# A two-layer hybrid backbone with a mixture of experts: the layout of the expert weight slots in SBUF

## The chip, the cores and the metric

The kernel runs on one core of a Trainium2 chip. The metric is the device time in microseconds of one execution, the median of three. Five engines work beside each other on the core, each with its own stream of instructions: TensorE (PE: matmuls and turnings, with PEld for its weight loads), VectorE (DVE), ScalarE (ACT), GpSimd (POOL) and SyncE (SP, which issues nearly all transfers). 16 DMA engines move the data. The engines wait for each other on semaphores.

## The reference

All data are fp32. There are 256 latent tokens and 256 context tokens of width 1024, and two layers. In each layer:

```
h  = modulate(rms_norm(x, g_mix), sh1, sc1)       # six modulation vectors = silu(c) @ w_ada + b_ada
z  = h @ w_in                                     # conv, two attentions, three gates
x += gt1 * (sum_i sigmoid(gate_i) * (o_i @ w_branch_i)) @ w_out
h2 = modulate(rms_norm(x, g_ffn), sh2, sc2)
aff = softmax(h2 @ w_router)                      # 16 experts; each picks its best 32 tokens of 256
xe = h2[idx]                                      # (expert, 32, 1024)
a, u = xe @ w_exp_gate[e], xe @ w_exp_up[e]       # 1024 x 1024 each, as is w_exp_down
ye = ((silu(a) * u) @ w_exp_down[e]) * gate       # added back to the tokens that were picked
x += gt2 * ye
```

The first layer does this for the latent and the context tokens, the second for the latent ones alone. The result is `rms_norm(x, g_final)` of the latent tokens.

## The kernel before

`make_plan` writes one list of steps for each layer, and every engine walks the same list and does its part of each step. Up to the experts a layer is dense work: `w_ada` and `w_in` blocks come through a ring in SBUF; each block is split into two fp32r parts (`WH`, `WL`, lines 1008 and 1183) and multiplied three times (lines 1535 to 1537).

The step `moe` is the expert stage. One expert has three matrices of 1024 x 1024, 4 MiB each. They are loaded as six slots of 2 MiB (`SLOT` is 4096 words on each of 128 partitions): slots 0 and 1 hold w_exp_gate, 2 and 3 w_exp_up, 4 and 5 w_exp_down. In a slot, partition p holds rows p, 128 + p, 256 + p and 384 + p of the 512 rows, 4 KiB each. SP loads the six slots of expert 0 while the dense work ends (line 874), then, in a loop over the experts 1 to 15, waits for `chunk_used[j]` and loads slot j again (line 878). All of these transfers lie in one queue, in that order.

TensorE (line 1641 on) takes the experts four at a time (`g`), with `eo` from 0 to 3 inside. `product` multiplies the gathered tokens (`XEB`, the stationary operand) with the rows of a slot, which stream past as the moving operand, and counts `chunk_used[j]` up at a slot's last matmul. G column groups of the array work at once, each on 1024 / G columns of the result: G is 2 in layer 0 (64 token slots, latent and context) and 4 in layer 1 (32 token slots). After gate and up, ScalarE and VectorE form silu(a) * u in `HID`, TensorE turns it by blocks of 128 columns (line 1670), ScalarE copies the result to `HIDT` (line 1128), and the down product follows. VectorE scales it into `YE` (line 1448). After four experts TensorE adds all of them back to the tokens by a matmul with `STB` (line 1686) and VectorE adds that to `X` (line 1457).

Before the stage come the norm (`norm` with `which` 1, lines 991 and 1221: XN = X * RS, by halves of 512 columns, half of the token tiles on each of ScalarE and VectorE), the turning of XN (line 1518), the routing and the gathering (line 1626). The order of the rows of `XE`, of the modulation vectors and of `w_router` on the partitions must be that of the weight rows.

At the start, SP loads the constants and small vectors: `CONST` (rows of 7296 bytes) and rows of `ROWS`, which TensorE turns into the columns `COLS`; then `w_ada`, `x`, `ctx`, `w_router` (line 855), `sw_sink` and `w_in`.

## Time and profile before

| | |
|---|---|
| median of 3 runs | 2038.43 us (2038.4 to 2043.76) |
| span of the profiled execution | 2033.6 us, first to last instruction |
| median less span | 4.8 us |
| mean granted TensorE clock | 0.933 |
| busy, share of the span | PE 78%, PEld 48%, DVE 36%, ACT 24%, POOL 5% |
| moved by DMA | 544.77 MB, 268 GB/s in the mean |
| chain that ended last | PE 37%, SP's queue 26%, DMA 13%, DVE 13%, ACT 7% |

No time of its own is recorded for the profiled execution, so its span stands for it. Busy shares are means over stages with different limits. The page cuts the span into 40 slices of 50.8 us, and windows can be asked for; the chain of waits goes back from the last instruction, at each step to what released it. A transfer's time in it runs from issue to landing. "SPq" is SP's queue: the time in which SP was issuing. The DMA share is the packets' summed time over that of 16 engines and can pass 1, where packets overlap.

### The profile page before, as it was taken

How to read it: one execution, taken by the hardware profiler on the slowest of the kernel's cores; microseconds unless marked ns; L12 is line 12 of the kernel's file. 1: busy time of each engine (PE TensorE's matmuls, PEld its weight loads, DVE VectorE, ACT ScalarE, POOL GpSimd, SP SyncE). 2: the span in 40 equal slices, each digit the busy share in tenths (PEclk: the TensorE clock that was granted, in tenths of full speed). 3: DMA queues.
4: the chain of work that ended last, by engine and by line, in shares of the span. 5: the costliest groups of instructions: out<-in, count | busy, mean ns of one | idle time of the engine just before them, and what ended most of it. 6: DMA issues, size and time to landing. Idle time of an engine off the chain costs nothing.

```text
span 2033.6 us, 25423 instructions
## 1 busy us (share of the span) xinstructions
PE 1587.8 (78%) x10052; PEld 979.6 (48%) x10052; DVE 737.2 (36%) x1597; ACT 487.0 (24%) x1051; POOL 102.1 (5%) x149
## 2 busy tenths in 40 slices
PE   4999999889986978787787799889786565555654
PEld 1887777666664322222222598777673222222221
DVE  3356665655434112121211556766553010100102
ACT  3225555541242000000000435555250000000000
POOL 1002200000001000000000102200000000000000
PEclk8999999999997999999999899989988888888887
DMA  9332231126853999999999643345775999999996
GB/s 340 109 93 86 81 93 38 63 83 229 280 215 144 410 409 410 410 410 410 410 410 410 204 145 90 118 144 199 245 278 220 408 409 410 410 410 410 409 410 256
DMA packets 225060, 544.77 MB, mean 268 GB/s; under 512 B 8990, under 2 KB 99300, under 8 KB 224980
## 3 DMA queue, kind: packets, MB, share of 16 engines
q1 hardware_dynamic: 222580, 537.53, 69.9%
q0 software_dynamic: 2400, 6.16, 1.0%
q8 instruction: 52, 0.85, 0.2%
q14 instruction: 28, 0.23, 0.0%
HBM read 540.68 MB, written 2.98 MB: 267 GB/s over the span
## 4 chain that ended last, share of the span: by engine, by line
PE 37%; SPq 26%; DMA 13%; DVE 13%; ACT 7%; issue 5%; POOL 0%; DVEq 0%; POOLq 0%; ACTq 0%
SPq L878 25%; DMA ring<-in_w_exp_down 9%; PE bank L1658 7%; PE bank L1535 7%; PE bank L1537 7%; PE bank L1536 7%; DVE WL L1183 3%; PE bank L1686 3%; PE bank L1496 2%; DMA ring<-in_w_in 2%; ACT WH L1008 1%; PE bank L1626 1%; ACT PB L1081 1%; DMA ring<-in_w_ada 1%; DVE PB L1333 1%
## 5 line engine op out<-in xcount | busy, mean ns | idle before, releaser
L1658 PE MATMUL bank<-ring,XEB 128*32 128x256 f32 (+1 forms) x3072 | 392.1, 514 | 184.5 <-DMA ring<-in_w_exp_up 98.3
L1658 PEld LDWEIGHTS bank<-ring,XEB 128*32 128x32 f32 (+1 forms) x3072 | 143.8, 135 | 431.1 <-issue 174.3
L1535 PE MATMUL bank<-HH,WH 128*128 128x512 f32 (+1 forms) x864 | 308.0, 357 | 5.1 <-DVE WL L1183 4.5
L1536 PE MATMUL bank<-HL,WH 128*128 128x512 f32 (+1 forms) x864 | 303.5, 351 | 0.0
L1537 PE MATMUL bank<-HH,WL 128*128 128x512 f32 (+1 forms) x864 | 303.0, 351 | 0.0
L1658 PE MATMUL bank<-ring,HIDT 128*32 128x256 f32 (+1 forms) x1536 | 199.4, 522 | 79.0 <-DMA ring<-in_w_exp_down 67.6
L1183 DVE TENSOR_TENSOR WL<-ring,WH 128x1024 fp32r<-128x1024 f32 (+1 forms) x172 | 184.9, 1077 | 177.2 <-ACT WH L1008 176.5
L1008 ACT CAST WH<-ring 128x1024 fp32r<-128x1024 f32 (+1 forms) x172 | 158.0, 924 | 136.5 <-DMA ring<-in_w_in 59.6
L1535 PEld LDWEIGHTS bank<-HH,WH 128*128 128x128 f32 x864 | 167.1, 193 | 39.0 <-issue 14.5
L1448 DVE TENSOR_TENSOR YE<-bank,GT 32x512 f32<-32x512 f32 (+1 forms) x128 | 70.9, 554 | 301.1 <-PE bank L1658 299.8
L1537 PEld LDWEIGHTS bank<-HH,WL 128*128 128x128 f32 x864 | 166.7, 193 | 21.3
L1536 PEld LDWEIGHTS bank<-HL,WH 128*128 128x128 f32 x864 | 167.0, 193 | 20.3
L1658 PEld LDWEIGHTS bank<-ring,HIDT 128*32 128x32 f32 (+1 forms) x1536 | 73.9, 137 | 188.1 <-issue 78.4
L1125 ACT ACTIVATE TH<-bank 128x512 f32<-128x512 f32 (+1 forms) x32 | 15.7, 490 | 579.8 <-PE bank L1658 579.8
L1442 DVE TENSOR_TENSOR HID<-TH,bank 128x512 f32<-128x512 f32 (+1 forms) x32 | 17.7, 554 | 262.2 <-PE bank L1658 262.2
L1438 DVE SCALAR_TENSOR_TENSOR TH<-TH,bank 128x512 f32<-128x512 f32 (+1 forms) x32 | 17.7, 554 | 236.3 <-ACT TH L1125 236.3
L1128 ACT ACTIVATE HIDT<-bank 128x512 f32<-128x512 f32 (+1 forms) x32 | 15.7, 490 | 319.1 <-PE bank L1670 319.1
L1535 PE MATMUL bank<-OH,WH 128*128 128x512 f32 (+1 forms) x192 | 67.6, 352 | 7.3 <-DVE OL L1366 3.9
L1496 PE MATMUL bank<-ring,CS 128*32 128x512 f32 x384 | 51.1, 653 | 25.3 <-ACT GT L1056 12.8
L1686 PE MATMUL bank<-YE,STB 128*128 128x512 f32 x96 | 52.4, 692 | 20.5 <-DVE YE L1448 20.5
L1080 ACT ACTIVATE PB<-PB,SM 128x256 f32<-128x256 f32 x64 | 32.6, 509 | 139.5 <-DVE SM L1336 139.5
L1571 PE MATMUL bank<-CONST,PB 128*128 128x128 f32 x320 | 53.3, 282 | 15.8 <-DVE PB L1360 15.8
(190 smaller groups left out, 1782.2 us busy)
## 6 DMA issues: line engine op xcount, KB each, us to landing
ring<-in_w_exp_gate SPq DMA_DIRECT2D x64, 2048.0 KB, 23.5
ring<-in_w_exp_up SPq DMA_DIRECT2D x64, 2048.0 KB, 23.6
ring<-in_w_exp_down SPq DMA_DIRECT2D x64, 2048.0 KB, 23.7
ring<-in_w_ada SPq DMA_DIRECT2D x48, 1024.0 KB, 7.2
ring<-in_w_in SPq DMA_DIRECT2D x40, 1024.0 KB, 5.6
ring<-in_w_in SPq DMA_DIRECT2D x28, 512.0 KB, 4.9
ring<-in_w_branch SPq DMA_DIRECT2D x24, 512.0 KB, 6.2
ring<-in_w_out SPq DMA_DIRECT2D x8, 1024.0 KB, 7.9
```

What stands on the lines that cost most here:

```text
L878: sp.dma_start(place(SLOT * j, (4, D)), expert_chunk(bass.ds(e, 1), j)).then_inc(expert_in[j], 16)
L1008: nc.scalar.copy(WH[b.b % NWS][:, 0:b.kk, :], w).then_inc(split_hi, 1)
L1080: nc.scalar.activation(p_[:, 0:SEQ], p_[:, 0:SEQ], ACT.Exp, bias=NM[u2], accum_out=ES[u2][:, 0:1])
L1183: nc.vector.tensor_tensor(WL[b.b % NWS][:, 0:b.kk, :], w, WH[b.b % NWS][:, 0:b.kk, :].bitcast(f32), ALU.subtract).then_inc(split_lo, 1)
L1448: last = nc.vector.tensor_tensor(YE[32 * eo:32 * eo + 32, q, nw * c:nw * c + nw], YAB[rows, 0:nw], GT2[32 * eo:32 * eo + 32, q, nw * c:nw ...
L1496: last = mm(t[32 * j:32 * j + 32, :], CS[:, 2 * j + kk, :], w[j // 2][:, 2 * (j % 2) + kk, :], start=kk == 0, stop=kk == 1, tile_position= ...
L1535: mm(t, wh, hi[:, k, 0:b.n], start=k == 0, stop=False)
L1536: mm(t, wh, lo[:, k, 0:b.n], start=False, stop=False)
L1537: last = mm(t, wl, hi[:, k, 0:b.n], start=False, stop=k == b.kk - 1)
L1571: last = nc.tensor.transpose(TB[x.u % 2][:, 128 * c:128 * c + 128], PB[x.u % 2][:, 128 * c:128 * c + 128], IDENT)
L1658: last = mm(out_bank[tw * c:tw * c + tw, 0:nw], stationary[:, k, 0:tw], w[:, nw * c:nw * c + nw], start=k == 0, stop=k == KD - 1, tile_pos ...
L1686: mm(SCB[i % 2][:], STB[:, q, 128 * j:128 * j + 128], YE[:, q, 512 * h:512 * h + 512], start=True, stop=True).then_inc(sc_ready, 1)
```

## The change

Each slot is laid out so that partition p holds the four consecutive rows 4p to 4p + 3 of the 512 rows, 16 KiB that are one run in DRAM and one in SBUF. Since the contraction runs over (partition, k), every operand that meets these weights takes the same order:

- the norm before the experts writes XN in the order (k, q) from X in the order (q, k), by `xn_half`;
- the shift, scale and g_ffn vectors of that norm are turned at every fourth column (`MB`, `ROWS3`); three constant transfers take the place of one, and there are four small turnings more at the start;
- `w_router` is loaded as two groups of four consecutive rows on a partition, 256 bytes a run in place of 64;
- for the hidden units, layer 0 turns `HID` at every fourth column; layer 1 keeps blocks of 128 columns in the turning, and there the gate and up products read the weights at every fourth column (`spread`), column group c making the hidden units 4n + c.

The down product's columns and everything after it stay as they are.

```diff
-        NROW2 = 16 + DEPTH * 12
-        COLS = sb("COLS", [128, 128 + NROW2], region(4 * (128 + NROW2)))
+        NROW1, NROW2, NROW3 = 112, 16 + DEPTH * 12, 12
+        C_COND, C_CONV, C_FFN = NROW1, NROW1 + 16, NROW1 + NROW2
+        NCOLS = NROW1 + NROW2 + 4 * NROW3
+        COLS = sb("COLS", [128, NCOLS], region(4 * NCOLS))
         ROWS = sb("ROWS", [128, 2, 128], R_P)
+        ROWS3 = sb("ROWS3", [NROW3, 512], R_P + 1024)
...
+        def xn_half(tt, c, which):
+
+            dst, src = XN[:, tt, 512 * c:512 * c + 512], X[:, tt, 512 * c:512 * c + 512]
+            if which == 1:
+                return dst.rearrange("p (k q) -> p k q", k=4), src.rearrange("p (q k) -> p k q", k=4)
+            return dst, src
...
-            sp.dma_start(ROWS[112:128, 0, :], A["g_ffn"].rearrange("l (r p) -> (l r) p", p=128)).then_inc(const_in, 16)
+            for l in range(DEPTH):
+                sp.dma_start(ROWS3[4 * l:4 * l + 4, :], A["b_ada"][l, SH2 * D:GT2V * D].rearrange("(r n) -> r n", n=512)).then_inc(const_in, 16)
+            sp.dma_start(ROWS3[8:12, :], A["g_ffn"].rearrange("l (r n) -> (l r) n", n=512)).then_inc(const_in, 16)
...
-                                sp.dma_start(WR[:, l_, :, :], A["w_router"][l_].rearrange("(k p) e -> p k e", p=128)).then_inc(late_const_in, 16)
+                                sp.dma_start(WR[:, l_, :, :].rearrange("p (h k) e -> p h k e", k=4), A["w_router"][l_].rearrange("(h p k) e -> p h k e", p=128, k=4)).then_inc(late_const_in, 16)
...
                         def expert_chunk(e, j):
-                            return mats[j // 2][e, 512 * (j % 2):512 * (j % 2 + 1), :].rearrange("a (k p) n -> p (a k) n", p=128)
+                            return mats[j // 2][e, 512 * (j % 2):512 * (j % 2 + 1), :].rearrange("a (p k) n -> p (a k n)", k=4)
...
-                                sp.dma_start(place(SLOT * j, (4, D)), expert_chunk(bass.ds(e, 1), j)).then_inc(expert_in[j], 16)
+                                sp.dma_start(ring[:, SLOT * j:SLOT * j + SLOT], expert_chunk(bass.ds(e, 1), j)).then_inc(expert_in[j], 16)
...
-                            last = nc.scalar.activation(XN[:, tt, 512 * c:512 * c + 512], X[:, tt, 512 * c:512 * c + 512], ACT.Copy, scale=RS[:, tt:tt + 1])
+                            last = nc.scalar.activation(*xn_half(tt, c, s.which), ACT.Copy, scale=RS[:, tt:tt + 1])
...
-                                nc.scalar.activation(HIDT[:, :, 0:tw].rearrange("p (h c) t -> p c h t", h=G),
-                                                     HTB[:, 0:8 * tw].rearrange("p (c h t) -> p c h t", h=G, t=tw), ACT.Copy, scale=0.5).then_inc(hidt_ready, 1)
+                                hidt = HIDT[:, :, 0:tw].rearrange("p (h c) t -> p c h t" if G == 2 else "p (c h) t -> p c h t", h=G)
...
-                                last = nc.vector.tensor_scalar(XN[:, tt, 512 * c:512 * c + 512], X[:, tt, 512 * c:512 * c + 512], RS[:, tt:tt + 1], None, ALU.mult)
+                                last = nc.vector.tensor_scalar(*xn_half(tt, c, s.which), RS[:, tt:tt + 1], None, ALU.mult)
...
+                        for k in range(4):
+                            last = nc.tensor.transpose(t[:, C_FFN + NROW3 * k:C_FFN + NROW3 * k + NROW3], ROWS3[:, k::4], IDENT[0:NROW3, 0:NROW3])
...
-                                last = nc.tensor.transpose(t[:, 128 * k:128 * k + 128], MB[:, 128 * k:128 * k + 128], IDENT)
+                                cols = slice(k, 512, 4) if s.v in (SH2, SC2) else slice(128 * k, 128 * k + 128)
+                                last = nc.tensor.transpose(t[:, 128 * k:128 * k + 128], MB[:, cols], IDENT)
...
-                                        last = mm(out_bank[tw * c:tw * c + tw, 0:nw], stationary[:, k, 0:tw], w[:, nw * c:nw * c + nw],
+                                        last = mm(out_bank[tw * c:tw * c + tw, 0:nw], stationary[:, k, 0:tw], w[:, c::G] if spread else w[:, nw * c:nw * c + nw],
...
-                                product(GAB[eo % 2], XEB[eo % 2], 0, e0)
-                                product(UAB[eo % 2], XEB[eo % 2], 2, e0)
+                                product(GAB[eo % 2], XEB[eo % 2], 0, e0, G == 4)
+                                product(UAB[eo % 2], XEB[eo % 2], 2, e0, G == 4)
...
-                                    last = nc.tensor.transpose(HTB[:, 128 * c:128 * c + 128], HID[:, 128 * c:128 * c + 128], IDENT)
+                                    cols = slice(c, 512, 4) if G == 2 else slice(128 * c, 128 * c + 128)
+                                    last = nc.tensor.transpose(HTB[:, 128 * c:128 * c + 128], HID[:, cols], IDENT)
```

## Rows read from the trace of the kernel before

**Rows 1.** The page's 40 slices of the span: DMA share, GB/s.
```profile
DMA  9332231126853999999999643345775999999996
GB/s 340 109 93 86 81 93 38 63 83 229 280 215 144 410 409 410 410 410 410 410 410 410 204 145 90 118 144 199 245 278 220 408 409 410 410 410 410 409 410 256
```

**Rows 2.** Windows, core 0: us, busy us by engine (count), PEclk, DMA share, GB/s.
```profile
700.00:800.00 100.00, 81.30 (x350) 25.62 (x346) 20.62 (x30) 4.11 (x7) 2.34 (x4) 1.00 1.03 409
1700.00:1800.00 100.00, 57.57 (x650) 26.10 (x654) 10.33 (x22) 2.30 (x6) 1.49 (x4) 0.83 1.03 410
```

**Rows 3.** Chain of waits, layer 1's expert stage: start us, us, what.
```profile
1742.88 23.75 DMA ring<-in_w_exp_down
...
1865.76 23.75 DMA ring<-in_w_exp_down
```

**Rows 4.** DMA view, 1700 to 1800 us, 4 KiB rows.
```profile
DMA packets 10304, 40.96 MB, mean 410 GB/s; under 512 B 304, under 2 KB 304, under 8 KB 10304
```

**Rows 5.** DMA view, 20 to 30 us, w_ada in 2 KiB rows.
```profile
DMA packets 1823, 3.89 MB, mean 389 GB/s; under 512 B 63, under 2 KB 63, under 8 KB 1823
```

**Rows 6.** DMA view, 44 to 46 us, w_in in 1 KiB rows.
```profile
DMA packets 691, 0.70 MB, mean 349 GB/s; under 512 B 16, under 2 KB 690, under 8 KB 690
```

**Rows 7.** DMA view, 3 to 4 us, constants: queue, packets, MB, share.
```profile
q1 hardware_dynamic: 56, 0.41, 96.7%
```

**Rows 8.** Timelines, ends of both expert stages: start us, us, instructions [idle before].
```profile
658.05 3.80 SPq L878 DMA_DIRECT2D ring<-in_w_exp_gate  x2
...
1122.59 3.65 PE L1658 MATMUL bank<-ring,HIDT 128*64 128x512 f32 x16 [0.81 <-DMA ring<-in_w_exp_down]
...
1545.61 7.11 PE L1658 MATMUL bank<-ring,XEB 128*32 128x256 f32 x128 [1.73 <-POOL XEB L953]
...
1547.75 2.10 SPq L878 DMA_DIRECT2D ring<-in_w_exp_gate  x2
...
2012.40 3.41 PE L1658 MATMUL bank<-ring,HIDT 128*32 128x256 f32 x32 [3.06 <-DMA ring<-in_w_exp_down]
...
2017.86 5.39 PE L1686 MATMUL bank<-YE,STB 128*128 128x512 f32 x8 [2.04 <-DVE YE L1448]
```

**Rows 9.** Timeline, layer 1, one expert's up slots and first down slot.
```profile
1812.75 1.93 PE L1658 MATMUL bank<-ring,XEB 128*32 128x256 f32 x32 [1.72 <-DMA ring<-in_w_exp_up]
...
1817.87 3.40 PE L1658 MATMUL bank<-ring,XEB 128*32 128x256 f32 x32 [3.19 <-DMA ring<-in_w_exp_up]
...
1823.08 1.93 PE L1658 MATMUL bank<-ring,HIDT 128*32 128x256 f32 x32 [0.82 <-DMA ring<-in_w_exp_down]
```

**Rows 10.** Chain of waits, layer 0, around the end of four experts.
```profile
876.82 3.68 PE bank L1658 x16
...
883.56 7.71 PE bank L1686 x16
...
892.27 13.97 PE bank L1658 x64
...
908.35 7.11 PE bank L1658 x32
```

**Rows 11.** Timeline of SP's queue at the start.
```profile
3.33 0.30 SPq L842 DMA_DIRECT2D ROWS<-in_conv_w  x1
...
21.94 7.78 SPq L855 DMA_DIRECT2D WRP<-in_w_router  x2
29.76 3.54 SPq L856 DMA_DIRECT2D SINK<-in_sw_sink  x1
```

**Rows 12.** Chain of waits at the start.
```profile
33.41 5.89 DMA ring<-in_w_in
```

**Rows 13.** Timeline, layer 0, the norm before the experts.
```profile
604.94 2.56 ACT L991 ACTIVATE XN<-X,SM 128x512 f32<-128x512 f32 x4 [1.11 <-DVE SM L1160]
604.94 1.67 DVE L1221 TENSOR_SCALAR XN<-X,SM 128x512 f32<-128x512 f32 x4
```

**Rows 14.** Groups by line, turning of the modulation halves.
```profile
L1508 PE MATMUL bank<-CONST,MB 128*128 128x128 f32 x80 | 12.4, 277 | 4.8 <-DVE MB L1187 4.8
```

More of the change, by code:

```diff
@@ L824, in wait_released @@
                     engine.wait_ge(split_lo, o.split_end)
+        def xn_half(tt, c, which):
[3 more added lines that the diff above has]
+            return dst, src
         def bcast_rows(row):
             return bass.AP(tensor=row.tensor, offset=row.offset, ap=[[0, 128]] + list(row.ap))
-        NCONST = 7
+        NCONST = 9
         block = ctx.enter_context(nc.Block())
@@ L873, in _ @@
                                 sp.wait_ge(blk_ready, s.c_tile if j < (4 if l == 0 else 5) else s.d_tile)
[L874 removed]
+                            sp.dma_start(ring[:, SLOT * j:SLOT * j + SLOT], expert_chunk(slice(0, 1), j)).then_inc(expert_in[j], 16)
                         with sp.Fori(1, NE) as e:
@@ L998, in _ @@
                         act.wait_ge(blk_ready, s.tile.ready)
-                        link(nc.scalar.copy(COLS[:], BLK[s.tile.bank][:, 0:128 + NROW2]))
-                        nc.scalar.activation(TC, COLS[:, 128:144], ACT.Tanh, scale=0.5).then_inc(act_evicted, 1)
+                        link(nc.scalar.copy(COLS[:], BLK[s.tile.bank][:, 0:NCOLS]))
+                        nc.scalar.activation(TC, COLS[:, C_COND:C_CONV], ACT.Tanh, scale=0.5).then_inc(act_evicted, 1)
                     elif kind == "split":
@@ L1126, in _ @@
                                 act.wait_ge(hid_turned, g * 4 + (TURN0 + e0 + 1))
-                                nc.scalar.activation(HIDT[:, :, 0:tw].rearrange("p (h c) t -> p c h t", h=G),
-                                                     HTB[:, 0:8 * tw].rearrange("p (c h t) -> p c h t", h=G, t=tw), ACT.Copy, scale=0.5).then_inc(hidt_ready, 1)
+                                hidt = HIDT[:, :, 0:tw].rearrange("p (h c) t -> p c h t" if G == 2 else "p (c h) t -> p c h t", h=G)
+                                nc.scalar.activation(hidt, HTB[:, 0:8 * tw].rearrange("p (c h t) -> p c h t", h=G, t=tw), ACT.Copy,
+                                                     scale=0.5).then_inc(hidt_ready, 1)
                     elif kind == "final":
@@ L1175, in _ @@
                         dve.wait_ge(act_evicted, s.tile.act)
-                        link(nc.vector.scalar_tensor_tensor(T2, TC, 1.0, COLS[:, 128:144], ALU.add, ALU.mult))
+                        link(nc.vector.scalar_tensor_tensor(T2, TC, 1.0, COLS[:, C_COND:C_CONV], ALU.add, ALU.mult))
                         nc.vector.tensor_scalar(CS[:, :, 0:2].rearrange("p k s -> p s k"), T2.rearrange("p (s k) -> p s k", s=2),
@@ L1203, in _ @@
                             c0 = 48 * s.l + 8 * s.v + 4 * s.half
-                            bias = COLS[:, c0:c0 + 4].unsqueeze(2).broadcast_to((128, 4, 2))
+                            bias = COLS[:, c0:c0 + 4]
+                            ffn = COLS[:, C_FFN:NCOLS].rearrange("p (k r) -> p r k", r=NROW3)
+                            if s.v in (SH2, SC2):
+                                bias = ffn[:, 4 * s.l + 2 * (s.v - SH2) + s.half, :]
+                            bias = bias.unsqueeze(2).broadcast_to((128, 4, 2))
                             add = nc.vector.tensor_tensor(m, RED, bias, ALU.add)
@@ L1212, in _ @@
                                 link(add)
-                                c0 = (96 if s.v == SC1 else 112) + 8 * s.l + 4 * s.half
-                                g = COLS[:, c0:c0 + 4].unsqueeze(2).broadcast_to((128, 4, 2))
+                                c0 = 96 + 8 * s.l + 4 * s.half
+                                g = COLS[:, c0:c0 + 4] if s.v == SC1 else ffn[:, 8 + 2 * s.l + s.half, :]
+                                g = g.unsqueeze(2).broadcast_to((128, 4, 2))
                                 link(nc.vector.tensor_scalar(m, m, 1.0, None, ALU.add))
@@ L1250, in _ @@
                                 dve.wait_ge(o_ready, b.o_ready - 1)
-                            tap = [COLS[:, 144 + 12 * l + 4 * k + b.i:145 + 12 * l + 4 * k + b.i] for k in range(3)]
+                            tap = [COLS[:, C_CONV + 12 * l + 4 * k + b.i:C_CONV + 1 + 12 * l + 4 * k + b.i] for k in range(3)]
                             ct = CT[:, 0:ns, :]
@@ L1484, in _ @@
                         t = open_tile(s.tile)
-                        nc.tensor.transpose(t[:, 0:128], ROWS[:, 0, :], IDENT)
-                        nc.tensor.transpose(t[:, 128:128 + NROW2], ROWS[0:NROW2, 1, :], IDENT[0:NROW2, 0:NROW2]).then_inc(blk_ready, 1)
+                        nc.tensor.transpose(t[:, 0:NROW1], ROWS[0:NROW1, 0, :], IDENT[0:NROW1, 0:NROW1])
+                        nc.tensor.transpose(t[:, NROW1:C_FFN], ROWS[0:NROW2, 1, :], IDENT[0:NROW2, 0:NROW2])
+                        for k in range(4):
+                            last = nc.tensor.transpose(t[:, C_FFN + NROW3 * k:C_FFN + NROW3 * k + NROW3], ROWS3[:, k::4], IDENT[0:NROW3, 0:NROW3])
+                        last.then_inc(blk_ready, 1)
                         pe.wait_ge(cs_ready, 1)
@@ L1648, in _, with product @@
                         with pe.Fori(0, 4) as g:
-                            def product(out_bank, stationary, j0, e0, ready=None):
+                            def product(out_bank, stationary, j0, e0, spread):
                                 for k in range(KD):
@@ L1673, in _ @@
                                 pe.wait_ge(ye_ready, g * 4 + (YE0 + e0))
-                                product(YAB, HIDT, 4, e0)
+                                product(YAB, HIDT, 4, e0, False)
                             pe.wait_ge(stb_ready, g + (4 * l + 1))
```

1 line of the change is left out of this document (removed).

## The prediction

> **What bounds the kernel now.** I read the page's slices first [rows 1]: the DMA lines show two long stretches at 410 GB/s, about 660 to 1125 us and 1560 to 2012 us, and 38 to 280 GB/s in between. They are the expert stages of the two layers. The windows [rows 2] say who is late there: TensorE is busy 81 and 58 us in 100, the DMA engines all the time. The chain of waits of layer 1 [rows 3] agrees: the same transfer of w_exp_down is issued at 1742.88 and at 1865.76. That is four experts of six slots, 24 slots in 122.88 us, 5.120 us for one slot of 2 MiB, or 409.6 GB/s. So each expert stage is a stream of weights, and TensorE waits for each slot. How many slots the end hangs on: the first six are loaded during the stage before. In layer 0 the first refill goes out at 658.05 and the last slot is consumed from 1122.59; 90 slots x 5.120 = 460.8 us lead to 1118.9, so 3.7 us are start. In layer 1 it is 1547.75, 2008.6 and 2012.40, 3.8 us of start [rows 8]. In all, 180 slots lie one after the other on the path.
>
> **What one packet costs.** The change makes 128 rows of 16 KiB out of 512 rows of 4 KiB in each slot, so the question is what a packet costs beyond its bytes. Three saturated stretches with one row size each tell: 1 KiB rows 349 GB/s [rows 6], 2 KiB rows 389 [rows 5], 4 KiB rows 409.6 [rows 3, 4]. With 16 engines that is 16 x 1024 / 349 = 46.9 ns, 84.2 ns and 160.0 ns for a packet. The line through the first and the last has a slope of (160.0 - 46.9) / 3072 = 0.0368 ns a byte and leaves 9.2 ns for the packet; at 2 KiB it gives 84.6, and 84.2 was seen. Does it hold above 4 KiB? The constants' rows of 7296 bytes are the only large ones of this queue: 56 packets in 1 us at a share of 96.7% is 16 x 0.967 / 56 = 276 ns each [rows 7], and the line says 277.8. So I take it to 16 KiB: 9.2 + 603.2 = 612 ns, eight of them on each engine: 4.90 us for a slot, 428 GB/s. The saving is 24 packets x 9.2 ns = 0.22 us a slot.
> The Trainium skill (DMA: Bandwidth & Descriptors, Why small descriptors are slow) has a smaller price, about 3 cycles a packet, and (Where 436 GB/s comes from) a ceiling of 16 x 32 B at 850 MHz. Three cycles are 3.5 ns, and the estimate by that page would be 180 x 24 x 3.5 ns = 15 us saved. The slope above is 27.2 GB/s an engine, which is the ceiling; the 9.2 ns are not the 3 cycles. Four row sizes lie on one line here, so the sum goes by them.
>
> **The change part by part.**
> 1. The stream: 180 x 0.22 = -40 us, half in each layer. Bounds: 0, if the engine still pays for each 4 KiB, and -180 x 0.30 = -54 if the 16 KiB packets cost nothing beyond bytes; -40 is taken.
> 2. Gate and up weights of layer 1 are now read by TensorE at every fourth word (`w[:, c::G]`). A slot of 32 matmuls takes 1.93 us, or 3.40 us on TensorE's lower clock, to which it falls behind a wait of some 3 us (0.83 is the mean granted clock of the stage, between the levels of 1.2 and 2.4 GHz) [rows 2, 9]; unhindered, 128 take 7.11 us, 1.78 a slot [rows 8]. No row shows TensorE reading SBUF with a step. At the lower end it costs nothing. What hides more: with s for such a slot, one expert costs TensorE 4s, two down slots of 1.93, about 1.8 us from the last up slot to the first down matmul (HID, turning, HIDT; 1821.27 to 1823.08) [rows 9], and a fourth of the 7.4 us that combining takes (2015.8 to 2023.3) [rows 8]: 4s + 7.5. This stays under 6 x 4.90 = 29.4 up to s = 5.5 us, three times today's. I take 3.6 us (twice): hidden, but for the first slot of the stage, which is freed 1.8 us later, and its refill starts the stream: between 0 and +1.8, +1 taken. A busier TensorE would also keep the higher clock for longer, which I count as nothing. From above: four times, the rival below.
> 3. Layer 0's weight reads are unchanged, and only HID is turned at every fourth column, within the 2.1 us between gate and up (to 906.24) and down (908.35). The unhindered expert is 13.97 + 2.1 + 7.11 = 23.2 us, with a fourth of the group's end (from 880.50, where the down slot of 876.82 ends, to 892.27: 11.8 us) 26.1 us [rows 10]. Even with the 2.1 us doubled it stays under 29.4. Here the cover is 3.3 us, the thinnest; if it went, slots would be freed late.
> 4. `xn_half` reads X at every fourth word before each expert stage, where TensorE waits for it and DMA is nearly done: all on the path. Before: 4 on ScalarE in 2.56 us and 4 on VectorE in 1.67 us, side by side; layer 1 has half as many [rows 13]. If VectorE falls from 0.42 to ScalarE's 0.64 us for one, its four end where ScalarE's do, at no cost. Bounds: 0, and +2.6 and +1.3 if ScalarE takes twice as long. Taken: +1 for both.
> 5. The turning of the modulation halves for SH2 and SC2 reads MB with a step: 8 x 4 matmuls of 12.4 / 80 = 0.155 us [rows 14] in stages that TensorE bounds. 0 to +5 (twice), 0 taken; VectorE's bias additions only change addresses.
> 6. The start. Two more constant transfers at about 0.4 us of SP each ahead of the first w_ada load (conv_w goes out at 3.33), so all w_ada loads go out later: +0.8. Four small turnings and a wider copy into COLS add well under 1 us, hidden, since the first w_ada matmul waits for its own transfer. Against it: the router weights take 2 x 1024 rows of 64 bytes now, and SP is held 7.78 us by them and 3.54 us by SINK behind them, because its queue is full and each issue waits for room (in the expert stage 23.75 us, 4.6 slots, lie between issue and landing [rows 3]). So the first w_in load goes out only at 33.41 and lands 5.89 us later, at 39.3, and ScalarE's first split waits for it, on the path [rows 11, 12]. With 2 x 256 rows of 256 bytes SP gets by 7.78 x 3/4 = 5.8 us earlier at the least, w_in follows w_ada with no gap: 1 MiB at 349 GB/s is 3 us [rows 6], from about 34 to 37: -2.3. Bounds: -3 and 0. Net of the start: -1.5.
> 7. Queues: a slot's issue is held on SP by the full queue, not by a slot in use; with a quarter of the descriptors SP gets ahead, up to the six slots. No gain of its own, as the DMA engines never idle there. The loads of layer 1 and the last GF load follow the stream as before.
>
> Sum: -40 + 1 + 1 - 1.5 = -39.5. The profiled span is 2033.6 us; the median of the runs is 2038.4, 4.8 more for what lies around the span. Span after 2033.6 - 39.5 = 1994; time 1998 to 1999. I say **1998.5 us**.
>
> **Rivals.**
> *The packet price doesn't fall* (same). If the engine handles a 16 KiB row as four 4 KiB pieces, or reading is what limits, slots stay at 5.12 us and only the small terms remain: 2038.4 + 0.5 = 2039. Against it: 7296-byte rows lie on the line. For it: no row shows 16 KiB. Chance 0.08.
> *TensorE becomes layer 1's bound* (slower). If a step of four words costs as much as reading all four, s = 4 x 1.78 = 7.1 us, and the expert 28.5 + 7.5 = 36 us; it decides from s = 5.5 us. Sixteen of them from 1545.6 - 21 = 1524.6 end at 2101, plus the 10.3 us that follow combining today: span 2111, time about 2116. For it: the stream already reads four column groups at once. Against it: 8192 columns in each group in 7.11 us are 1.15 a ns, 2.1 cycles of 2.4 GHz for a column [rows 8], which may cover a slower fetch. Chance 0.12.
> The Trainium skill (SBUF — State Buffer, Door 1: The DMA port swizzle, SBUF "cachelines") says that lines are 16 bytes and that full rate needs two hits in a line; a step of four words has one. It names no price and calls a step of up to four fp32 free in the same paragraph. No row here shows it.
> *Part of the gain is eaten*: s near 5.5 or a saving of 4 to 5 ns a packet, with items 4 and 5 at their upper ends. 2010 to 2030. Chance 0.08.
>
> **The numbers.** Forecast 0.72, with its own range of 1992 to 2006: the stream at -42 to -36, items 2, 4 and 5 up to +6 more, the start between -3 and +1. Range 1990 to 2032: forecast and the partial case, 0.80 together. Beyond 0.3% (6 us, about what a measurement of this kernel can tell): faster 0.80, within 0.08, slower 0.12.
>
> **What would show it.** DMA at 428 GB/s in both stretches and a slot every 4.90 us; 128 packets a slot; the last w_exp_down consumed about 21 us earlier in layer 0 and 41 us earlier in layer 1. TensorE's gate and up slots of layer 1 give s. ScalarE's first split at about 37.5. XN's rows give item 4. It would be wrong if a slot took 5.12 us still, or if DMA fell below a full share in layer 1.

## The result and the profile after

The changed kernel takes 2007.97 us (median of 4 runs, 2007.45 to 2008.78), the kernel before, timed beside it, 2041.06 (4 runs, 2038.40 to 2043.76): ratio 0.9837, 95% interval 0.9823 to 0.9851, 33 us faster. Two later sets of five runs gave 0.9825 [0.9812, 0.9839] and 0.983 [0.9817, 0.9843]. The direction was as forecast. The time lies in the stated range of 1990 to 2032 us, but 2 us above the 1992 to 2006 that the prediction gave its main forecast; 1998.5 us was 9.5 us too low. One later run of the kernel before took 3976.13 us, in a slow state, and is left out of every figure below.

Five views of the changed kernel's profile answer to the rows of before. First the page's slices and two windows of the expert stages (columns as in [rows 2]):

```profile
DMA  9332331116765799999999643335665999999996
GB/s 352 104 94 71 94 93 43 56 50 211 267 225 210 298 427 428 428 428 429 429 428 428 216 140 108 121 127 190 230 245 206 427 427 429 428 428 429 428 428 254
```
```profile
700.00:800.00 100.00, 85.33 (x358) 28.35 (x359) 18.66 (x28) 4.18 (x7) 2.34 (x4) 0.97 1.01 428
1700.00:1800.00 100.00, 72.53 (x666) 23.19 (x662) 10.74 (x23) 2.68 (x7) 1.49 (x4) 0.95 1.01 429
```

428 GB/s where [rows 1] had 410, with the DMA share still full: the engines move the same bytes in less time, and they are still what bounds both stages. In layer 1 TensorE's busy time went from 58 to 73 us in 100, and its mean granted clock from 0.83 to 0.95. The DMA view of the second window counts the packets, 2940 for 42.88 MB where [rows 4] had 10304 for 40.96:

```profile
DMA packets 2940, 42.88 MB, mean 429 GB/s; under 512 B 323, under 2 KB 323, under 8 KB 323
```

Now TensorE's timeline in layer 1, two gate slots, two up slots and the first down slot of one expert (it answers to [rows 9]):

```profile
1814.43 3.81 PE L1680 MATMUL bank<-ring,XEB 128*32 128x256 f32 x32 [2.96 <-DMA ring<-in_w_exp_gate]
1819.32 3.81 PE L1680 MATMUL bank<-ring,XEB 128*32 128x256 f32 x32 [1.09 <-DMA ring<-in_w_exp_gate]
1824.21 3.81 PE L1680 MATMUL bank<-ring,XEB 128*32 128x256 f32 x32 [1.08 <-DMA ring<-in_w_exp_up]
1829.11 3.81 PE L1680 MATMUL bank<-ring,XEB 128*32 128x256 f32 x32 [1.09 <-DMA ring<-in_w_exp_up]
...
1834.38 1.93 PE L1680 MATMUL bank<-ring,HIDT 128*32 128x256 f32 x32 [0.47 <-ACT HIDT L1141]
```

The starts lie 4.89 or 4.90 us apart: that is the slot period. The strided gate and up slots take 3.81 us, the down slot, read without a step, 1.93 as before. Before each of these four strided slots TensorE still waits 1.08 us or more for the transfer.

What holds SP's issues has changed too. Between 1600 and 1950 us SP waited for TensorE to leave a slot 3 times, 3.9 us in all, before, and 71 times, 312.6 us in all, in the same window of the changed kernel: it now issues as far ahead as the six slots allow. The transfers still follow each other without a gap.

The ends of both stages, from the timelines (they answer to [rows 8]; the group at 1536.28 is cut by its window after 80 of 128 matmuls, which take 14.69 us):

```profile
665.84 0.35 SPq L890 DMA_DIRECT2D ring<-in_w_exp_gate  x1
...
1110.18 3.65 PE L1680 MATMUL bank<-ring,HIDT 128*64 128x512 f32 x16 [0.33 <-DMA ring<-in_w_exp_down]
...
1536.28 9.25 PE L1680 MATMUL bank<-ring,XEB 128*32 128x256 f32 x80 [1.73 <-POOL XEB L965]
...
1540.30 3.96 SPq L890 DMA_DIRECT2D ring<-in_w_exp_gate  x2
...
1985.71 3.48 PE L1680 MATMUL bank<-ring,HIDT 128*32 128x256 f32 x32 [2.58 <-DMA ring<-in_w_exp_down]
...
1991.24 5.39 PE L1709 MATMUL bank<-YE,STB 128*128 128x512 f32 x8 [2.05 <-DVE YE L1466]
```

From the first refill to the last slot: 444.34 us in layer 0 (464.54 before) and 445.41 in layer 1 (464.65), 39.4 us less together. The spans fell by 26.6 us only, from 2033.6 to 2007.0, so 12.8 us were lost elsewhere between these two executions. One piece is in these rows: the first slot of layer 1 is freed 4.02 us after its matmuls begin, where it was 2.14. Others are in the norm before the experts, layer 0 and then layer 1 ([rows 13] is layer 0 before; layer 1 before had 1.33 and 0.88):

```profile
610.92 4.53 ACT L1003 ACTIVATE XN<-X,SM 128x512 f32<-128x512 f32 x4 [1.11 <-DVE SM L1173]
610.92 2.43 DVE L1239 TENSOR_SCALAR XN<-X,SM 128x512 f32<-128x512 f32 x4
...
1506.09 2.32 ACT L1003 ACTIVATE XN<-X,SM 128x512 f32<-128x512 f32 x2 [1.09 <-DVE SM L1173]
1506.09 1.26 DVE L1239 TENSOR_SCALAR XN<-X,SM 128x512 f32<-128x512 f32 x2
```

and at the start, SP's queue, ScalarE's first split and the last of TensorE's four w_ada products ahead of it (they answer to [rows 11, 12]; the w_in row is cut by its window):

```profile
3.85 0.30 SPq L854 DMA_DIRECT2D ROWS<-in_conv_w  x1
...
22.21 4.06 SPq L867 DMA_DIRECT2D WRP<-in_w_router  x2
26.31 1.31 SPq L868 DMA_DIRECT2D SINK<-in_sw_sink  x1
32.16 1.00 SPq L861 DMA_DIRECT2D ring<-in_w_in  x2
```
```profile
34.00 3.13 PE L1517 MATMUL bank<-ring,CS 128*32 128x512 f32 x16
```
```profile
37.48 1.99 ACT L1020 CAST WH<-ring 128x1024 fp32r<-128x1024 f32 x2 [8.26 <-DMA ring<-in_w_in]
```

### The profile page after: what moved, and what is told of

The parts are those of the page before. It is cut to its first block, busy times and chain, and to the rows that moved or that the text cites. A ratio compares the mean times of both kernels' runs of the same rounds, so it can differ in the third digit from the quotient of the medians.

```text
span 2007.0 us, 25433 instructions
## 1 busy us (share of the span) xinstructions
PE 1670.2 (83%) x10056; PEld 978.1 (49%) x10056; DVE 738.2 (37%) x1597; ACT 489.9 (24%) x1051; POOL 101.9 (5%) x149
## 4 chain that ended last, share of the span: by engine, by line
PE 44%; DMA 31%; DVE 13%; ACT 7%; issue 4%; SPq 0%; POOL 0%; DVEq 0%; ACTq 0%; POOLq 0%
DMA ring<-in_w_exp_down 28%; PE bank L1680 14%; PE bank L1557 7%; PE bank L1559 7%; PE bank L1558 7%; DVE WL L1196 3%; PE bank L1517 2%; PE bank L1709 2%; DMA ring<-in_w_in 2%; ACT WH L1020 1%; PE bank L1648 1%; ACT PB L1093 1%; DMA ring<-in_w_ada 1%; DVE PB L1351 1%; DVE SM L1353 1%
## 5 line engine op out<-in xcount | busy, mean ns | idle before, releaser
L1680 PE MATMUL bank<-ring,XEB 128*32 128x256 f32 (+1 forms) x3072 | 470.6, 620 | 101.0 <-DMA ring<-in_w_exp_gate 50.6
L1680 PE MATMUL bank<-ring,HIDT 128*32 128x256 f32 (+1 forms) x1536 | 187.7, 488 | 54.2 <-DMA ring<-in_w_exp_down 35.7
L1680 PEld LDWEIGHTS bank<-ring,HIDT 128*32 128x32 f32 (+1 forms) x1536 | 67.9, 126 | 155.9 <-issue 67.3
L1517 PE MATMUL bank<-ring,CS 128*32 128x512 f32 x384 | 58.5, 736 | 23.2 <-ACT GT L1068 12.2
```

The costliest lines, as they stand in the source:

```text
L1517: last = mm(t[32 * j:32 * j + 32, :], CS[:, 2 * j + kk, :], w[j // 2][:, 2 * (j % 2) + kk, :], start=kk == 0, stop=kk == 1, tile_position= ...
L1680: last = mm(out_bank[tw * c:tw * c + tw, 0:nw], stationary[:, k, 0:tw], w[:, c::G] if spread else w[:, nw * c:nw * c + nw], start=k == 0, ...
```

## Experiments

Each was timed beside the kernel before. Four numbers per kernel, read from its timelines, carry most of what follows: A, the first prefetch issue of layer 0's experts (all dense products of layer 0 but the last lie ahead of it); B, from the first refill to the start of the last slot's matmuls in layer 0; C, the same in layer 1; D, from the start of layer 1's last slot's matmuls to the end of the span. In the kernel "twice" the last two slots run as one group; its C and D are taken at the start of that group, 1.8 us before the last slot. The medians are of all runs of a kernel, the letters of one profiled execution. Times in us.

| kernel | median | A | B | C | D |
|---|---|---|---|---|---|
| before, profile of the forecast | | 584.77 | 464.54 | 464.65 | 21.2 |
| before, second profile | 2042.40 | 588.69 | 464.57 | 464.64 | 21.3 |
| changed, three profiles | 2007.97, 2005.87, 2008.41 | 590.77, 590.88, 590.69 | 444.3 to 444.4 | 445.3 to 445.4 | 21.3 |
| stream only | 2000.26 | 589.68 | 444.32 | 444.98 | 18.2 |
| changed, 4 KiB rows | 2044.62 | 590.70 | 464.70 | 464.56 | 20.5 |
| changed, 8 KiB rows | 2016.34 | 586.73 | 451.60 | 451.34 | 22.0 |
| no strided weight reads | 2002.81 | 588.87 | 444.60 | 445.18 | 18.2 |
| XN plain | 2002.75 | 587.41 | 444.38 | 445.39 | 19.7 |
| XN mostly on VectorE | 2005.52 | 591.50 | 444.36 | 445.17 | 19.7 |
| MB plain | 2004.51 | 587.96 | 444.45 | 445.30 | 21.3 |
| twice | 2078.11 | 591.18 | 444.61 | 513.24 | 20.0 |
| router only | 2040.18 | 588.57 | 464.81 | 465.32 | 18.3 |

### The changed kernel again

> The changed kernel itself once more, beside the others on one chip. Both theories: 2006 to 2009 us and 0.984 of the kernel before. Theory A (the missing 13 us of the dense stages are the edits' own cost) and theory B (most of them are TensorE's clock, which falls at other places) agree here; B expects that the clock falls at the same places of the dense stage of layer 0 as in the first profile, since the kernel is the same.

Measured: 2005.87 (2002.46 to 2006.87), ratio 0.9825 [0.9812, 0.9839]. It is the measure for the next three. The expectation of theory B on the clock came true: from 150 to 170 us the mean granted clock is 0.83 in both profiles (and in the third), and A is 590.88 for 590.77. So in layer 0 the executions of this kernel that were profiled did not differ; in layer 1's dense stage, from the last slot of layer 0 to the first refill of layer 1, they did: 430.12, 427.46 and 430.12 us.

### The transfers alone

```diff
--- before
-mats[j // 2][e, 512 * (j % 2):512 * (j % 2 + 1), :].rearrange("a (k p) n -> p (a k) n", p=128)
+mats[j // 2][e, 512 * (j % 2):512 * (j % 2 + 1), :].rearrange("a (p k) n -> p (a k n)", k=4)
-sp.dma_start(place(SLOT * j, (4, D)), expert_chunk(...))
+sp.dma_start(ring[:, SLOT * j:SLOT * j + SLOT], expert_chunk(...))
```

> The kernel before with nothing changed but the transfers of the expert slots: 16 KiB rows (the weights meet operands in the wrong order, so the numbers of the experts are wrong). Packet theory: a slot every 4.90 us in both layers, 180 x 0.223 = 40 us less than before, and s stays at 1.8 to 1.9 us. If the dense stages lose time by their strided reads and the new start (theory A), they lose nothing here and the whole 40 us come out: 1998 to 2001 us. If the clock's place is chance (theory B), the dense stages may still lose or win 3 to 6 us: 1995 to 2006. Rival (the gain comes from the strided kernel's busier TensorE or from the operand order): a slot stays at 5.12 us.

Measured: 2000.26 (1998.49 to 2001.53), ratio 0.9804 [0.9791, 0.9818], 5.6 us less than the changed kernel. Its DMA view from 1680 to 1780 us:

```profile
DMA packets 2941, 42.88 MB, mean 429 GB/s; under 512 B 324, under 2 KB 324, under 8 KB 324
```

The stream's gain is all here: B and C are 20.2 and 19.7 us shorter than before. The rest of the change costs 5.6 us by the medians; 3.0 of them lie in D, where the two kernels do the same work (see the last section).

### The size of a row

```diff
--- changed: 4 KiB rows
-.rearrange("a (p k) n -> p (a k n)", k=4)      # and ring[:, ...] as the target
+.rearrange("a (k p) n -> p (a k) n", p=128)    # and place(SLOT * j, (4, D))
--- changed: 8 KiB rows, row 256h + 2p + k on partition p
```

> The changed kernel with the slots' transfers in 4 KiB rows as before (order of the expert weights wrong). Packet theory: 5.12 us a slot again, so 180 x 0.223 = 40 us more than the changed kernel: about 2047 to 2048 us, which is 5 to 9 us slower than the kernel before, the price of all the other edits together. Rival (the other edits cost nothing by themselves): the same as the kernel before, 2038 to 2041.

Measured: 2044.62 (2043.48 to 2045.29, 11 runs), ratio to before 1.0015 [1.0006, 1.0024], 38.8 us more than the changed kernel, which is the packet theory's 40. It expected the other edits to cost 5 to 9 us over the kernel before. Measured are 2.6 us (1.2 to 4.9 by the interval): less than that, and more than the rival's nothing. From 1680 to 1780 us:

```profile
DMA packets 10307, 40.96 MB, mean 410 GB/s; under 512 B 307, under 2 KB 307, under 8 KB 10307
```

> The changed kernel with 8 KiB rows (two consecutive rows on a partition; order of the expert weights wrong). Packet theory: 16 packets of 9.2 + 301.6 = 310.8 ns on each engine, 4.97 us a slot, 422 GB/s, 180 x 0.075 = 13 us more than the changed kernel: about 2021 us. Rival (there is a step at 4 KiB: any larger row is as good as the largest, or only a whole slot in one run is better): 4.90 or 5.12 us a slot, 2008 or 2048 us.

Measured: 2016.34 (2015.45 to 2019.46), ratio 0.9885 [0.987, 0.99], 10.5 us more than the changed kernel. From 1680 to 1780 us:

```profile
DMA packets 5471, 42.20 MB, mean 422 GB/s; under 512 B 320, under 2 KB 320, under 8 KB 320
```

By 16 engines, a packet of 8 KiB takes 16 x 8192 / 422 = 310.6 ns, one of 16 KiB 16 x 16384 / 428.5 = 611.8; the prediction's line gives 9.2 + 301.6 = 310.8 and 612.4. By the stage length B, which is sharper than the time: (464.70 - 444.34) / 90 slots / 24 packets = 9.4 ns, and from 4 to 8 KiB (464.70 - 451.60) / 90 / 16 = 9.1. So the price is one per packet, the same within 0.3 ns from 4 to 16 KiB, and neither rival's slot time occurs: 2 MiB at 422 GB/s are 4.97 us. B and C differ by 7.3 + 6.0 = 13.3 us, as forecast. The medians differ by 10.5 only; in the profiled execution A was 4 us early, with the same dense work, but whether the other three runs had that too is not recorded.

### Layer 1 without strided weight reads

```diff
--- changed
-product(GAB[eo % 2], XEB[eo % 2], 0, e0, G == 4)
-product(UAB[eo % 2], XEB[eo % 2], 2, e0, G == 4)
+product(GAB[eo % 2], XEB[eo % 2], 0, e0, False)
+product(UAB[eo % 2], XEB[eo % 2], 2, e0, False)
```

The changed kernel, timed beside the next three, first:

> The changed kernel once more, as the measure beside its three variants of the same rounds. Expected 2004 to 2008 us. Its own stages should stay at what the two traces showed: ScalarE's four XN half-tiles about 4.5 us in layer 0 and 2.3 in layer 1, the layer-1 first slot some 4.0 us of TensorE from the last of the stage's start to the first refill. If two profiles of this one kernel again differ by some us in the dense stages, with the same work in them, the difference lies in the clock of the execution and not in the change.

Measured: 2008.41 (2004.57 to 2010.02), ratio 0.983 [0.9817, 0.9843]. ScalarE's XN rows take 4.54 and 2.32 us and the first slot of layer 1 is freed after 4.02 us, as expected.

> The changed kernel with the layer-1 gate and up products reading contiguous columns again (the hidden columns of layer 1 come out in another order, so layer 1's expert numbers differ; the work is the same in count and size). Theory A (the strided reads cost only the first slot, since the stream hides the rest): 1.9 us less than the changed kernel, a slot's 32 matmuls back at 1.8 to 2.0 us, the slot period of layer 1 unchanged at 4.90 us, TensorE's share in the stage down from 72 to about 58 in 100. Rival B (the strided reads also hold up releases in the steady state): more than 4 us less, and a shorter period than 4.90 us. Rival C (a busier TensorE keeps its own clock up and pays for the strided reads): the granted clock of the stage falls to about 0.83 again and the time is within 1 us of the changed kernel's.

Measured: 2002.81 (1998.56 to 2004.90), ratio 0.9813 [0.98, 0.9826]. The windows from 1680 to 1780 us, the changed kernel's and then this one's:

```profile
1680.00:1780.00 100.00, 71.36 (x668) 23.37 (x664) 10.76 (x23) 2.69 (x7) 1.90 (x5) 0.95 1.01 429
```
```profile
1680.00:1780.00 100.00, 61.18 (x686) 26.93 (x686) 12.01 (x26) 2.31 (x6) 1.49 (x4) 0.80 1.01 428
```

The first slot is freed in 2.14 us again, 1.88 less, and C is the same within 0.2 us: theory A for the strided reads. The medians differ by 5.6 us, more than its 1.9, which would be rival B's size; but B's mechanism, earlier releases in the stream, is not there. The rest lies where the two kernels have the same work: in the profiled executions A is 1.8 us smaller, and D 3.0. Rival C's first half is right (the clock falls back to 0.80) and its second wrong: in this stage the clock decides nothing, since the transfers end last at either level.

### The turned norm

```diff
--- XN plain, from the changed kernel
-            if which == 1:
+            if which == 9:
--- XN mostly on VectorE, from the changed kernel (ScalarE: one half-tile, signals 2)
-for c in range(2):
-    for tt in range(s.ntt // 2, s.ntt):
+for c in range(1 if s.which == 1 else 2):
+    for tt in range(s.ntt - 1 if s.which == 1 else s.ntt // 2, s.ntt):
...
-for tt in range(s.ntt // 2):
+for tt in range(s.ntt - (c == 0) if s.which == 1 else s.ntt // 2):
```

> The changed kernel with the XN half-tiles ahead of the experts written in plain order again (the columns of XN then do not match the order of the weights, the work is the same in count and size). Theory A (the turned XN costs what ScalarE needs longer for its four and two half-tiles, on the path to the first refill): ScalarE back at 2.56 us and 1.33 us, 2.0 and 1.0 us earlier first refills, 3 us less in all. Rival B (the wait goes to something else at once, such as TensorE's clock or the transfers of the first six slots): less than 1 us less in all, although ScalarE's rows are short again.

> The changed kernel with the turned XN work divided anew: ScalarE does one half-tile, VectorE (0.61 us for one, against 1.13 on ScalarE) all others. In layer 0 the last half-tile is then done after 7 x 0.61 = 4.3 us instead of 4.5, in layer 1 after 3 x 0.63 = 1.9 instead of 2.3; but the first columns of XN are complete after four half-tiles each way, and TensorE takes them in order, so its start is what counts, and ScalarE is free for its evictions 3.4 us earlier. Theory A (the stage's path runs through ScalarE's evictions of the turned XN): 2 to 3 us less than the changed kernel. Rival B (it runs through the last XN half-tile): 0 to 0.6 us less. Rival C (VectorE's own next work, the other half of the evictions, is now late): up to 2 us more.

Measured: XN plain 2002.75 (2001.75 to 2006.53), ratio 0.9818 [0.9804, 0.9831]; mostly on VectorE 2005.52 (2004.53 to 2007.98), ratio 0.9827 [0.9814, 0.9841]. What counts is the time from the start of XN to XNL, which VectorE can only begin when TensorE and ScalarE are through with H. Timelines of layer 0: the changed kernel (its XN starts at 610.92, as shown above), XN plain, mostly on VectorE:

```profile
620.73 4.52 DVE L1391 TENSOR_TENSOR XNL<-XN,XNH 128x1024 fp32r<-128x1024 f32 x2 [2.68 <-PE bank L1540]
```
```profile
607.57 2.56 ACT L1003 ACTIVATE XN<-X,SM 128x512 f32<-128x512 f32 x4 [1.11 <-DVE SM L1173]
...
615.65 4.53 DVE L1391 TENSOR_TENSOR XNL<-XN,XNH 128x1024 fp32r<-128x1024 f32 x2 [2.92 <-PE bank L1540]
```
```profile
611.65 4.26 DVE L1239 TENSOR_SCALAR XN<-X,SM 128x512 f32<-128x512 f32 x7
611.71 1.21 ACT L1003 ACTIVATE XN<-X,SM 128x512 f32<-128x512 f32 x1 [1.17 <-DVE SM L1173]
...
620.12 4.53 DVE L1391 TENSOR_TENSOR XNL<-XN,XNH 128x1024 fp32r<-128x1024 f32 x2 [1.67 <-PE bank L1540]
```

9.81 us with the turned XN, 8.08 without (before: 604.94 to 612.91, 7.97), 8.47 with the new division. In layer 1 it is 5.28, 4.72 and 5.29 (before 4.73). So turning XN costs 1.8 + 0.6 = 2.4 us; the new division wins back 1.3 in layer 0 and nothing in layer 1. By the means of five runs it is 1.2 us under the changed kernel timed beside it (2006.1 and 2007.3), which the times alone don't tell from zero. For XN plain theory A had the place right, and 3 us where these rows give 2.4; the medians give 5.7 and the means of five runs 3.3 (2004.0 and 2007.3). For the new division its 2 to 3 us were about twice the 1.3 measured.

### How far TensorE's slack reaches

```diff
--- changed, inside product()
-for c in range(G):
+for c in [*range(G)] * (2 if spread and 0 < k < KD - 1 else 1):
```

> The changed kernel with six of the eight contraction steps of each layer-1 gate and up product done twice (the products come out too large; the transfers are the same). A slot's matmuls rise from 3.8 to 3.8 x 1.75 = 6.65 us, beyond the 5.5 us at which the prediction put the turn from the stream to TensorE. Theory A (its sum holds: four slots at s and 7.5 us for the rest): an expert takes 4 x 6.65 + 7.5 = 34.1 us instead of 29.4, layer 1 is bound by TensorE, 16 x 4.7 = 75 us more than the changed kernel, some 2080 us, the DMA share in layer 1 about 0.86. Rival B (TensorE has no slack to speak of, each added matmul shows at once): 16 x 4 x 2.85 = 182 us more. Rival C (the stream still covers it): within 10 us.

Measured: 2078.11 (2077.77 and 2078.45), ratio 1.0174 [1.0153, 1.0194], 71 us over the 2007.2 that is the median of the changed kernel's 14 runs, where theory A has 75. Window and timeline in layer 1:

```profile
1680.00:1780.00 100.00, 96.95 (x950) 34.82 (x946) 7.99 (x19) 2.68 (x7) 0.80 (x2) 1.00 0.98 398
```
```profile
1728.90 3.66 PE L1680 MATMUL bank<-ring,HIDT 128*32 128x256 f32 x64 [0.47 <-ACT HIDT L1141]
1732.38 25.66 PE L1680 MATMUL bank<-ring,XEB 128*32 128x256 f32 x224
1758.58 0.44 PE L1693 MATMUL bank<-CONST,HID 128*128 128x128 f32 x2 [0.54 <-DVE HID L1460]
1759.49 3.66 PE L1680 MATMUL bank<-ring,HIDT 128*32 128x256 f32 x64 [0.47 <-ACT HIDT L1141]
```

Now TensorE waits for no slot: four of them in 25.66 us, s = 6.4, and GB/s falls below the ceiling. The window lies inside a group of four experts; from 1540 to 2000 us it is a DMA share of 0.93 (about 0.86 expected) and 374 GB/s, 0.87 of 428. The prediction's formula gives 16 x (4 x 6.4 + 7.5) - 7.4 for the last combining = 522 us from the first matmul of the stage to the end of its last slot; measured are 1536.74 to 2056.72 + 3.66, 523.6 us. That it fits so well is in part luck: from one expert to the next inside a group it takes 30.5 us, where the formula has 31.3, and a group of four takes 11 to 12.5 us more than four times that, where it has 7.4. With the measured mean of 33.4 us an expert and s = 6.4, the turn from the stream to TensorE is worked out at s = 5.4 instead of 5.5; the runs themselves show only that 3.8 lies on one side and 6.4 on the other. So the rival "TensorE becomes layer 1's bound" was a real case, and s = 3.8 is well inside the bound.

### The second profile of before, and the small parts

> The kernel before, unchanged, for a second profile. The profile of before that the forecast was made from had 2033.6 us of span, while its timed runs were 2038.4 to 2044.8 and every later profile has only 1.6 to 1.8 us outside its span. Theory A (that one execution met fewer drops of the granted clock in its dense stages): a span of 2036 to 2043 us, the expert prefetch of layer 0 issued at 587 to 590 us instead of 584.8, the stream of each layer the same 464.5 us. Rival B (the dense stages of the changed kernel are really slower by 6 us ahead of the prefetch): prefetch within 1 us of 584.8, and a span near 2034.

Measured: one run, 2042.40, span 2040.6; A is 588.69, B and C are 464.57 and 464.64. Theory A: the profile that the forecast used was a quick execution. The two traces show where. SP's issues agree within 0.1 us up to 421 us (420.98 and 420.90); at the w_ada issue of 471.66 us in the first the second is 4.0 us later (475.64). In between, TensorE's mean granted clock was 1.00 in the first, and 0.83 from 440 to 460 us and 0.91 from 460 to 480 us in the second. Rival B is not quite done with: A of the changed kernel's three profiles is still 2.0 to 2.2 us later than that of this one.

```diff
--- router only, from before: w_router in 256-byte rows
-WR[:, l_, :, :] <- w_router[l_].rearrange("(k p) e -> p k e", p=128)
+WR[:, l_, :, :].rearrange("p (h k) e -> p h k e", k=4) <- w_router[l_].rearrange("(h p k) e -> p h k e", p=128, k=4)
--- MB plain, from the changed kernel
-cols = slice(k, 512, 4) if s.v in (SH2, SC2) else slice(128 * k, 128 * k + 128)
+cols = slice(128 * k, 128 * k + 128)
```

> The kernel before with nothing changed but the load of the router's weights, which comes in the changed kernel's order of rows (the routing numbers then come out otherwise, the work is the same). Theory A (it shortens the queue's hold at the start, but the first block of w_in then waits for TensorE to release its place): within 0.5 us of before, SyncE's router rows shorter by 3 to 4 us, and the first w_in issue at most 1.3 us earlier. Rival B (the prediction's item: the head of the queue sets the first product): 1.5 us less than before.

> The changed kernel with the modulation vectors turned in plain blocks of 128 columns (their order then does not match the experts' rows, the work is the same). Theory A (the strided transposes lie between other work of TensorE in the dense stages and cost 0.04 us for four): within 1 us of the changed kernel. Rival B (they are a part of the 6 us by which the changed kernel's dense stage of layer 0 was late): 2 us or more less, with the loss of SyncE's checkpoints between 150 and 570 us gone.

Measured: router only 2040.18 (2037.65 to 2042.82, 10 runs), ratio 0.999 [0.998, 0.9999]. The router's rows on SP took 3.81 us instead of 7.78 and w_in was issued at 32.17, both as theory A says; the time is 1.8 us less, as rival B says. The trace does not bear B out: the checkpoint of SP at 142.8 us is level with before (142.7), so what was won at the start is gone by then. Where the 1.8 us come from stays open; its profiled execution has D 3.0 us shorter than the second profile of before, and whether the other nine had that is not recorded. MB plain 2004.51 (2003.60 to 2006.43), ratio 0.9815 [0.9798, 0.9831]: against 0.983 of the changed kernel this does not decide, and A of 587.96 lies among those of kernels with the strided MB (586.73 to 591.50), so it does not speak for B either.

## Why the prediction was right, and where it was short

**The stream (item 1): right.** -40 forecast, 20.2 + 19.2 = 39.4 measured; 428 GB/s, 4.90 us a slot, 128 rows of 16 KiB. The line drawn through three row sizes at or below 4 KiB, and supported by the rows of 7296 bytes, held up to 16 KiB. The Trainium skill (DMA: Bandwidth & Descriptors, Why small descriptors are slow) would give 15 us, an estimate by its 3 cycles; the runs decide for 9.1 to 9.4 ns a packet.

**Strided weights (item 2): right in kind and price of a slot.** s was taken as 3.6 and is 3.81, the bound of 5.5 was not reached, and only the first slot shows. There the sum took +1, between 0 and +1.8; measured +1.88, the upper end, because that slot stands behind no transfer. With s taken as 3.6, the +1 contradicted its own term. That TensorE's own rate halves when it reads every fourth word agrees with the line rule of the Trainium skill (SBUF — State Buffer, Door 1: The DMA port swizzle, SBUF "cachelines"); but the same paragraph calls a step of up to four fp32 free, and for this read the measurement decides otherwise. The busier engine did keep the higher clock longer, 0.95 for 0.83, and it was worth nothing, as booked.

**The turned XN (item 4): mis-sized.** +1 taken for both layers, 2.4 measured. The sum took +1 between a lower bound at which only VectorE slows down (0) and an upper one at which ScalarE takes twice as long (3.9). ScalarE did slow down, by 1.8 times, and it is the later of the two: 0.64 to 1.13 us for one half-tile, VectorE 0.42 to 0.61. The upper bounds (+2.6, +1.3) held.

**HID and MB (items 3 and 5): hidden or small.** Turning HID in layer 0 hides: B is the same with it and without (444.3 in the changed kernel and in stream only). MB's cost was not resolved.

**The start (item 6): the queue moved, the lead was lost to the clock.** SP's hold by the router fell from 7.78 to 4.06 us and that by SINK from 3.54 to 1.31; SP was through both 5.7 us earlier (27.62 for 33.30), as the 5.8 of the prediction had it. Then it waited until 32.16 for a place in the ring, which a w_ada product of TensorE, ended at 32.11, sets free. The prediction looked at what was ahead in the queue and not at this wait behind it; still, the split came at 37.48 instead of 39.32, near the 37 forecast. What the sum left out is TensorE's clock. The next w_ada product ran at the lower level (3.13 us from 34.00; before, 1.92 from 34.12). The first product of w_in then starts 1.05 us earlier, but TensorE goes up to the higher level no earlier. Its matmuls, before and changed:

```profile
50.15 0.80 PE L1535 MATMUL bank<-HH,WH 128*128 128x512 f32 x1
...
52.84 0.40 PE L1535 MATMUL bank<-HH,WH 128*128 128x512 f32 x1
```
```profile
49.10 0.80 PE L1557 MATMUL bank<-HH,WH 128*128 128x512 f32 x1
...
53.54 0.40 PE L1558 MATMUL bank<-HL,WH 128*128 128x512 f32 x1
```

Six matmuls go at the lower level before and ten in the changed kernel; those start 0.43 us apart, the others 0.23, so four more of them cost 0.8 us. At the 27th matmul the lead is 0.20 us (57.22 for 57.42), and it is 0.19 at SP's issue at 142.49 (142.68 before). -1.5 was booked and no more than -0.2 shows in the two traces.

**The queues (item 7): right.** SP got ahead, up to the six slots, and waits for TensorE there (312.6 us of 350 in layer 1, 3.9 before). It brought no gain of its own: the DMA share was full before and after.

**The base: wrong by what one execution happens to be.** The prediction took 4.8 us outside the span, from 2038.4 - 2033.6. The runs with both numbers have 1.8 (2008.78 and 2007.0; 2042.40 and 2040.6). So the profiled execution of before took about 2035.4 us, less than any of 40 timed runs of that kernel (2038.40 to 2044.98, mean 2041.9), and the median of 2038.43 that the forecast started from, two of whose three runs are the two lowest of the 40, was on the low side.

**The sum again.** By stages: -39.4 + 1.9 + 2.4 = -35.1. By times: 14 runs of the changed kernel have a mean of 2006.7, 40 of before 2041.9: -35.2. The forecast's -39.5 was 4.4 too much, by the first slot (0.9), XN (1.4), the start (1.5) and the stream (0.6); its base was 3.5 too low. The other 1.6 us of the 9.5 are the difference of the first four runs' median from the mean of 14 (1.3) and rounding in the forecast. That the sum by stages and the means agree within 0.1 us is closer than either is known: the runs scatter by some 2 us each, D alone takes values from 18.2 to 22.0 us, and a cost of MB or HID in the dense stages of 1 to 2 us would not be seen. What the two traces give, 26.6 us, is not the effect of the change: the 8.5 us between it and the -35.1 lie in dense stretches, where the second profile of before is itself 7.0 us longer than the first (2040.6 and 2033.6). The forecast came as near as it did by the stream, 39.4 of the 40 us; the small terms all erred to the same side.

**The rivals.** "The packet price doesn't fall" is ruled out by B and C. "TensorE becomes the bound" needed s over 5.5 by the prediction; at 3.8 it does not occur, at 6.4 it does. "Part of the gain is eaten" is what happened on a small scale, by items 2, 4 and 6, not by an s near 5.5.

## What to carry to other kernels

Where the DMA engines are busy all the time, fit a line through the time of one packet at the row sizes that the trace already shows; its intercept times the packets saved is the forecast gain, and here it was right to 2%. Price a turned layout at its readers: the engine that ends later decides, and a read that was hidden in a stream is not hidden for the first slot. A lead won early can be lost to TensorE's clock a few us later. Split a difference between two traces by stage before you explain it, and take the base from many runs; one execution of this kernel can lie 6 us from the next.

## What the runs showed of the hardware that was not expected

A step of four words cost each of the three engines that read fp32 values with it here, each by its own factor: TensorE 1.78 to 3.69 us for 32 matmuls of 128x256 (7.11 us for 128 before, 14.75 for 128 from 1759.44 us after), ScalarE 0.64 to 1.13 us and VectorE 0.42 to 0.61 for 128x512.

For one kernel, the stream stages repeat within 0.15 us from execution to execution (B and C of before twice, of the changed kernel three times); the dense stages do not, with the same instructions: A is 584.77 and 588.69 in the two profiles of before, and 586.73 to 591.50 in nine profiles with the changed kernel's work up to A. In the changed kernel's profile TensorE has the lower clock for a part of 150 to 170 us (mean 0.83), in the profile of before it has 1.00 there, in the second profile of before too, in router only 0.83. No order of the kernels follows from it.

The end of the kernel runs at the lower level of TensorE's clock (1.2 GHz), at the higher (2.4 GHz) or across a change between them, and D goes from 18.2 to 22.0 us with it. The last slot's matmuls and the last combining in the second profile of before and in stream only:

```profile
2019.27 3.52 PE L1658 MATMUL bank<-ring,HIDT 128*32 128x256 f32 x32 [3.07 <-DMA ring<-in_w_exp_down]
2024.83 5.39 PE L1686 MATMUL bank<-YE,STB 128*128 128x512 f32 x8 [2.05 <-DVE YE L1448]
```
```profile
1978.49 1.93 PE L1658 MATMUL bank<-ring,HIDT 128*32 128x256 f32 x32 [1.43 <-DMA ring<-in_w_exp_down]
1982.46 3.88 PE L1686 MATMUL bank<-YE,STB 128*128 128x512 f32 x8 [2.04 <-DVE YE L1448]
```

Behind a wait of 3.07 us the last slot's matmuls ran at the lower level, behind one of 1.43 us at the higher: D is 21.3 us in the one and 18.2 in the other. Others lie between or above: 19.7 with the slot at the lower level and the combining at the higher (XN plain: 3.51 and 3.88 us), 22.0 with 8 KiB rows (3.10 and 6.54 us). The last wait alone does not decide it: in the changed kernel's profile the slot behind a wait of 2.58 us at 1985.71 took 3.48 us, and the one behind 2.60 us at 1809.54 took 1.93. So a difference in D can look like an effect of any edit before it. That it explains 3 of the 5.6 us by which stream only beats the changed kernel was read from the profiled executions; it was not tried by itself.
